# A two-layer hybrid decoder step: token rows of the expert stage by indirect transfers through DRAM tables

## The reference, cut to what matters

```
def swiglu(h, w_up, w_down):
    g, u = jnp.split(h @ w_up, 2, axis=-1)
    return (jax.nn.silu(g) * u) @ w_down

def moe_swiglu(h, w_router, w_up, w_down):
    logits = jnp.einsum('bld,de->ble', h, w_router, preferred_element_type=jnp.float32)
    top_v, top_i = lax.top_k(logits, TOP_K)
    top_w = jax.nn.softmax(top_v, axis=-1)
    combine = jnp.sum(top_w[..., None] * jax.nn.one_hot(top_i, N_EXPERTS, dtype=jnp.float32), axis=-2)
    ...
    for e in range(N_EXPERTS):
        out = out + combine[..., e:e + 1] * swiglu(h, w_up[e], w_down[e])
```

## Time and profile before

| | |
|---|---|
| median of three runs | 2266.97 us (2265.43 to 2270.44) |
| the profiled execution | 2268.26 us; span 2266.6 us |
| mean granted clock of TensorE | 0.992 of full speed |
| first expert slab asked for | 1306.66 us |
| expert products begin | 1320.29 us |
| last down product ends | 2252.7 us |
| DMA moved | 535.21 MB, mean 236 GB/s |

### The profile page before, as it was taken

How to read it: one execution, slowest core, us unless ns; L and a number is a source line. 1 busy time by engine, 2 the same in 40 slices (tenths; PEclk the granted TensorE clock), 3 DMA queues, 4 the chain that set the end, 5 groups by cost and what they waited for, 6 DMA issues and landing times.

```text
span 2266.6 us, 44485 instructions
## 1 busy us (share of the span) xinstructions
PE 2225.8 (98%) x19914; PEld 1410.3 (62%) x19914; DVE 621.5 (27%) x1229; ACT 386.3 (17%) x720; POOL 89.1 (4%) x138
## 2 busy tenths in 40 slices
PE   7999999999999999999999989999999999999999
PEld 6777777777777777777776744354444535353535
DVE  4394424432111128623353211111111020201011
ACT  3324333301000132342431110000000000000000
POOL 2001120000000000012000000000000000000000
PEclk9999999999999999999998999999999999999999
DMA  5335446464443543453476099999999899999993
GB/s 170 115 112 154 132 135 189 121 198 133 130 134 107 171 130 113 128 171 117 131 187 181 19 382 411 419 410 353 387 390 391 343 372 405 367 357 370 406 373 131
DMA packets 290397, 535.21 MB, mean 236 GB/s; under 512 B 10936, under 2 KB 222010, under 8 KB 273824
## 3 DMA queue, kind: packets, MB, share of 16 engines
q1 hardware_dynamic: 289836, 532.31, 66.5%
q10 hardware_dynamic: 372, 0.07, 0.0%
HBM read 518.50 MB, written 13.85 MB: 235 GB/s over the span
## 4 chain that ended last, share of the span: by engine, by line
PE 94%; DVE 3%; ACT 1%; issue 1%; DMA 1%; ACTq 0%; SPq 0%; DVEq 0%
PE bank L916 92%; PE bank L922 3%; ACT mem L1794 0%; DMA mem<-in_cache_kv_w_dram 0%; DVE mem L2521 0%; DVE col L2524 0%; DVE mem L2492 0%; DVE mem L2534 0%; DVE mem L2537 0%; ACTq L2103 0%; SPq L631 0%; DMA hv<-in_ssm_d_dram 0%; DVE mem L2213 0%; DVE mem L2217 0%; ACT hflat L1794 0%
## 5 line engine op out<-in xcount | busy, mean ns | idle before, releaser
L916 PE MATMUL bank<-mem 128*32 128x256 f32 (+10 forms) x11936 | 1033.7, 405 | 19.8 <-DVE mem L2860 5.4
L916 PEld LDWEIGHTS bank<-mem 128*32 128x32 f32 (+3 forms) x11936 | 606.2, 122 | 421.5 <-issue 231.6
L916 PE MATMUL bank<-hflat,mem 128*128 128x288 f32 (+1 forms) x2896 | 714.1, 407 | 0.0
L916 PEld LDWEIGHTS bank<-hflat,mem 128*128 128x128 f32 (+1 forms) x2896 | 536.0, 189 | 162.0 <-issue 19.3
L1794 ACT ACTIVATE mem<-bank 128x288 f32<-128x288 f32 (+8 forms) x384 | 171.2, 455 | 1135.3 <-PE bank L916 943.0
L916 PE MATMUL bank<-mem,steps 128*32 128x384 f32 (+1 forms) x3072 | 291.9, 539 | 0.0
L916 PEld LDWEIGHTS bank<-mem,steps 128*32 128x32 f32 x3072 | 98.6, 110 | 184.0 <-issue 183.2
L2213 DVE TENSOR_TENSOR xT<-xT,bank 128x288 f32<-128x288 f32 x72 | 28.4, 450 | 458.0 <-PE bank L916 458.0
L2217 DVE SCALAR_TENSOR_TENSOR mem<-mem,bank 128x288 f32<-128x288 f32 (+1 forms) x93 | 43.2, 479 | 214.7 <-ACT mem L1794 177.9
L1794 ACT ACTIVATE mem<-mem 128x1152 f32<-128x1152 f32 (+8 forms) x103 | 80.4, 780 | 100.3 <-DVE mem L2291 71.7
L922 PE MATMUL bank<-ident,mem 128*128 128x128 f32 (+3 forms) x570 | 80.0, 273 | 12.2 <-DMA mem<-in_x_sample_dram 7.1
(11 more groups left out here) (220 smaller groups left out, 749.2 us busy)
## 6 DMA issues: line engine op xcount, KB each, us to landing
mem<-in_w_moe_up_dram SPq DMA_DIRECT2D x64, 2048.0 KB, 11.2
mem<-in_w_moe_down_dram SPq DMA_DIRECT2D x56, 2048.0 KB, 11.2
mem<-in_w_moe_up_dram SPq DMA_DIRECT2D x32, 2304.0 KB, 9.7
mem<-in_w_in_dram SPq DMA_DIRECT2D x70, 1024.0 KB, 5.5
mem<-in_w_moe_up_dram SPq DMA_DIRECT2D x16, 1536.0 KB, 8.4
mem<-in_w_ffn_up_dram SPq DMA_DIRECT2D x44, 512.0 KB, 4.6
mem<-in_cache_kv_w_dram SPq DMA_DIRECT2D x26, 512.0 KB, 5.9
mem<-in_w_ffn_down_dram SPq DMA_DIRECT2D x16, 704.0 KB, 4.9
```

The lines of the kernel that those rows point to most:

```text
L916: return mm(out, lhsT, rhs, start=start, stop=stop, skip_group_check=True)
```

## The change

**Rows instead of matrices.** Two tables in DRAM, `xslots` and `yslots`, have 8 x 96 rows of 4 KB, one for each slot. DVE works out two slot numbers for each token (`to_slots`, 8 small instructions). POOL writes each token's normalised row to its two slots with six indirect DMAs (`put_rows`). ACT reads an expert's 96 rows with four DMAs (`load_rows`), DVE transposes them in 32 x 32 blocks to `hg` (`turn_expert`). The expert's output is stored to `yslots` with four DMAs (`store_rows`), and ACT waits until they have landed. When the last experts are done, POOL reads each token's two output rows back (`get_rows`: six DMAs while the last expert's down slabs run, three behind its store), and DVE adds them, weighted, to the residual in token rows `xrow`.

**What goes.** `gather`, `scatter`, the transposes of `Pc`, DVE's `Pm`, `Pc` and `add_scattered`, ACT's copies of `hg` and `Cm`, `turn_out` in the tail. The 24 transposes of `xT` now stand ahead of the loop (`turn_rows`), two blocks ahead of the rank products and one behind.

**What moves.** SP asks for expert slabs without knowing the number of rounds; each engine reads it inside the loop (`load_rounds` behind expert 0, on SP behind expert 1). PE raises `m_slab` by 16 ahead of the last branch projection of layer 1, which lets slabs 0 and 1 be asked for right behind the last `wo` slab, and by the other 5 behind the last `wo` product, which lets slabs 2 to 6 be asked for. In layer 0 SP fills the tables once (four DMAs, 3.5 MB from DRAM to DRAM), behind the stores of the key-value rows.

The diff, cut to its core (the bodies of `gather` and `scatter`, which go, stand in the code above):

```diff
+        hraw = view(arena, 3456, KT * CAP)
+        htok = view(arena, 6912, 3, D)
+        htokv = view(arena, 6912, 3, 4, KT * 32)
+        xrow = [xT[:, :, :].rearrange("p k t -> p (k t)")[:, D * b:D * b + D] for b in range(2)]
+        xrow.append(view(arena, 5888, D))
+        ylo = [eslot[0][:, 0:D], eslot[0][:, D:2 * D], eslot[1][:, 0:D]]
+        yhi = [eslot[0][:, 2 * D:3 * D], eslot[0][:, 3 * D:4 * D], eslot[1][:, D:2 * D]]
...
+        xslots = nc.dram_tensor("xslots", (NEXP * CAP, D), F32).ap()
+        yslots = nc.dram_tensor("yslots", (NEXP * CAP, D), F32).ap()
+        def slots_of(v, e):
+            return [v[CAP * e:CAP * e + CAP, 256 * q:256 * q + 256].rearrange("(p b) c -> p b c", b=TT) for q in range(4)]
+        def load_rounds(eng, end):
             eng.wait_ge(rounds_ready, 1)
-            return eng.value_load(rounds, min_val=1, max_val=-(-T // CAP))
+            eng.reg_load(end, rounds)
...
+                if L == 0:
+                    for i in range(3):
+                        sp.dma_start(xslots[TP * i:TP * i + TP, :], x_prompt[0]).then_inc(x_seeded, 16)
+                    sp.dma_start(yslots[CAP * (NEXP - 1):CAP * NEXP, :], x_prompt[0, 0:CAP, :]).then_inc(x_seeded, 16)
...
-            nr = load_rounds(sp)
-            with sp.Fori(0, nr) as r:
+            end = sp.alloc_register("sp_rounds")
+            with sp.Fori(0, end) as r:
...
+                    if e == 1:
+                        load_rounds(sp, end)
+                for b, (t0, n) in enumerate(BLK):
+                    dst = y_prompt[0, t0:t0 + n, :] if t0 < TP else y_sample.rearrange("b i d -> (b i) d")
+                    sp.wait_ge(y_added, 6 * r + 4 + b)
+                    sp.dma_start(dst, xrow[b][0:n, :]).then_inc(out_stored, 16)
...
+            def put_rows(dst, slots, src):
+                return gp.indirect_dma_start(dst, bass.IndirectOffsetOnAxis(ap=slots, axis=0), src, None,
+                                             bounds_check=last_row, oob_is_err=False)
...
+            pool.wait_ge(token_rstd, 1)
+            pool.wait_ge(tok_half0, 3)
+            for b, (t0, n) in enumerate(BLK):
+                half = htokv[0:n, b, :, 0:P]
+                step(gp.tensor_tensor(half, half, t_rstd[0:n, b:b + 1].unsqueeze(2).to_broadcast([n, 4, P]), ALU.mult))
...
+                pool.wait_ge(slots_ready, r + 1)
+                pool.sem_inc(pool_step, 1)
+                for b, (t0, n) in enumerate(BLK):
+                    for k in range(2):
+                        put_rows(xslots, slot_row[0:n, b, k:k + 1], htok[0:n, b, :]).then_inc(x_scattered, 16)
+                load_rounds(pool, end)
+                last = expert(r, NEXP - 1)
+                pool.wait_ge(y_out, 64 * last)
+                pool.wait_ge(*lat("m_slab", last, 16))
+                pool.sem_inc(pool_step, 1)
+                for b, (t0, n) in enumerate(BLK):
+                    get_rows(ylo[b][0:n, :], slot_row[0:n, b, 0:1], yslots).then_inc(lo_here[b], 16)
+                    get_rows(yhi[b][0:n, :], slot_early[0:n, b:b + 1], yslots).then_inc(hi_here[b], 16)
+                for b in range(3):
+                    pool.wait_ge(hi_here[b], 32 * r + 16)
+                    pool.sem_inc(pool_step, 1)
+                pool.wait_ge(y_out, 64 * last + 64)
+                pool.sem_inc(pool_step, 1)
+                for b, (t0, n) in enumerate(BLK):
+                    get_rows(yhi[b][0:n, :], slot_late[0:n, b:b + 1], yslots).then_inc(hi_here[b], 16)
...
+                if L == DEPTH - 1:
+                    pe.sem_inc(loop_signals["m_slab"], 16)
...
+            def turn_rows(b):
+                t0, n = BLK[b]
+                for k in range(2):
+                    acc = open_bank(("xrow", b, k))
+                    for i in range(4):
+                        ins = turn(acc[0:n, P * i:P * i + P], xT[:, 4 * k + i, t0:t0 + n])
+                    close_bank(ins, ("xrow", b, k))
             pe.wait_ge(*drained(("wo", 1, KT - 1)))
-            advance(pe, "m_slab")
+            pe.sem_inc(loop_signals["m_slab"], LOOP["m_slab"] - 16)
+            turn_rows(0)
+            turn_rows(1)
...
+            turn_rows(2)
+            for b in range(3):
+                for k in range(2):
+                    pe.wait_ge(*drained(("xrow", b, k)))
+            pe.wait_ge(*drained(("htok", 2, 1)))
...
-                        if n < 2 and e > 0:
-                            scatter(it - 1, n)
-                        if n == 2:
-                            pe.wait_ge(*lat("m_sel", it, 1))
-                            for b in range(TT):
-                                pe.wait_ge(*lat("m_added", it - 1, 5 + b))
-                                for tb, (t0, nt) in enumerate(BLK):
-                                    ins = turn(bank[up_bank[b]][:, t0:t0 + nt], Pc[0:nt, tb, b, :])
-                            ins.then_inc(*lup("m_turned"))
-                    pe.wait_ge(*lat("m_weights", it, TT))
+                    pe.wait_ge(*lat("m_hid", it - 1, 2 * TT))
...
-                        if n == 15 and e % 2 and e < NEXP - 1:
-                            gather_most(it + 1)
-                        if n == 18 and e % 2 and e < NEXP - 1:
-                            gather_rest(it + 1)
...
+            for b, (t0, n) in enumerate(BLK):
+                for k in range(2):
+                    key = ("xrow", b, k)
+                    copy_out(xrow[b][0:n, 512 * k:512 * k + 512], key, psum(key)[0:n, :])
...
+            def load_rows(e):
+                for q, src in enumerate(slots_of(xslots, e)):
+                    act.dma_start(hraw[32 * q:32 * q + 32, :].rearrange("p (b c) -> p b c", b=TT), src).then_inc(x_here, 16)
+            def store_rows(e):
+                for q, dst in enumerate(slots_of(yslots, e)):
+                    act.dma_start(dst, yb[32 * q:32 * q + 32, :, :]).then_inc(y_out, 16)
+            with act.Fori(0, end) as r:
+                act.wait_ge(x_scattered, 96 * (r + 1))
+                act.wait_ge(*lat("m_hgT", expert(r, 0) - 1, 1))
+                load_rows(0)
...
+                    if e < NEXP - 1:
+                        act.wait_ge(*lat("m_hgT", it, 1))
+                        load_rows(e + 1)
...
+                    act.wait_ge(*lat("m_y", it, 2))
+                    store_rows(e)
+                    act.wait_ge(y_out, 64 * it + 64)
...
+            def to_slots(step, done):
+                step(ve.tensor_scalar(near, rank2, 1.0, None, ALU.is_ge))
+                step(ve.scalar_tensor_tensor(near, rank2, float(CAP), near, ALU.is_le, ALU.mult))
+                step(tt(place, rank2, first_slot, ALU.add))
+                step(ve.scalar_tensor_tensor(slot_row, near, -OFF_END, place, ALU.mult, ALU.add))
+                step(tt(hi_at, place[:, :, 1], hi_7, ALU.add))
+                step(ve.scalar_tensor_tensor(slot_early, near[:, :, 1], -OFF_END, hi_at, ALU.mult, ALU.add))
+                step(ve.scalar_tensor_tensor(hi_at, place[:, :, 1], OFF_END, hi_7, ALU.add, ALU.subtract))
+                ins = ve.scalar_tensor_tensor(slot_late, near[:, :, 1], -OFF_END, hi_at, ALU.mult, ALU.add)
+                ins.then_inc(slots_ready, 1)
+                dve.wait_ge(slots_ready, done)
...
+                ve.scalar_tensor_tensor(xrow[b][0:n, :], rows[b][0:n, :], masked[0:n, b, k:k + 1], xrow[b][0:n, :],
+                                        ALU.mult, ALU.add).then_inc(y_added, 1)
...
+                def turn_expert(it, e):
+                    dve.wait_ge(x_here, 64 * (it + 1))
+                    ve.transpose(hg[e % 2].rearrange("p b k t -> p (b k t)"), hraw).then_inc(*lup("m_hgT"))
...
+                for b in range(3):
+                    dve.wait_ge(lo_here[b], 16 * (r + 1))
+                    add_expert(r, b, 0, ylo)
+                for b in range(3):
+                    dve.wait_ge(hi_here[b], 32 * (r + 1))
+                    dve.wait_ge(y_added, 6 * r + b + 1)
+                    add_expert(r, b, 1, yhi)
```

More of the change, by code:

```diff
@@ L45 @@
 CAP = 96
+OFF_END = 8192.0
 TT = CAP // 32
@@ L458, in hybrid_decoder @@
         for b in range(3):
[L459 to L460 removed]
+            for k in range(2):
+                job(("xrow", b, k), ((5, 6), (7, 3), (0, 1))[b][k])
         def filled(key):
@@ L1678, in _ @@
-            with pe.Fori(0, nr) as r:
-                gather_most(expert(r, 0))
-                gather_rest(expert(r, 0))
+            end = pe.alloc_register("pe_rounds")
+            with pe.Fori(0, end) as r:
                 for e in range(NEXP):
@@ L2130, in token_copies @@
                     key = ("htok", b, half)
-                    copy_out(htok[0:n, b, 512 * half:512 * half + 512], key, psum(key)[0:n, :])
+                    act.wait_ge(*filled(key))
+                    out = htokv[0:n, b, :, P * half:P * half + P].rearrange("t g (k f) -> t k g f", k=4)
+                    src = psum(key)[0:n, :].rearrange("t (k g f) -> t k g f", k=4, g=4)
+                    if half:
```

(17 more changed lines are left out.)

255 lines of the change are left out of this document (79 added, 176 removed).

## The result

The changed kernel takes 2232.85 us (median of four runs, 2230.22 to 2235.6) against 2266.51 for the kernel before beside it: a ratio of 0.9849, 95% interval 0.9831 to 0.9866. It is 34 us faster; 2219 was forecast, so the direction held and 14 us of the gain did not come. The profiled execution has a span of 2230.8 us, 35.8 less than before; by its own sum the prediction had 47.8 less.

A forecast was written before the change was run, and what follows sets the result against it. PE's own work was taken to bound the expert loop, with the feed close behind. Loop -62.0, rounds +1, head +11.8 and tail +1.4 gave -47.8 us from 2266.97: 2219 us, 8-in-10 range 2207 to 2240.

The forecast's parts named there:

- The loop: Expert loop: 62.0 us of gathers, scatters and transposes leave PE; 870.4 us left against 932.4, plus 1 us for rounds.
- (d): Head: rows landing beside slabs 2 to 6, forecast at 1325.5, between 1323 and 1333.
- (e): Head: ACT's four loads until 1329, DVE's turn 1.0 us; PE starts products at 1330.2, 9.9 us later than before.
- (a): Head: 16 transposes ahead of the rank products take 6.5 us, bounds 4.4 and 8.7; rank begins at 1308.2.
- (b): Head: rank products 2.2 us, then 11 small DVE instructions at 0.20 us; slots at 1312.8.
- (c): Head: six indirect DMAs on POOL at 1.3 us each, 7.8 us, last one out at 1320.6.
- (f): First products after PE's 18 us stop: 3.8 us at half speed, 1.9 us lost.
- The tail: Behind the expert loop: output stores, POOL's reads and DVE's multiply-add take 15.3 us, +1.4 against before.
- The filling of the tables: Layer 0: 3.5 MB read and written, 17 us at 415 GB/s, hidden behind wo slabs; nothing charged.
- The feed: Slab loading in the loop: 415 GB/s, rows cost 20 us in all, no stall; rival giving way a little 14%.
- 27 us to spare: Loop feed: 833 us needed of 860 us, so it holds while it keeps 402 GB/s.
- The sentence on the early request: Slabs asked for early: takes nothing off the path by itself, as PE did not wait for a slab before.

The follow-up runs named there:

- e3: Changed kernel without row loads for experts 1 to 7 and output stores of experts 0 to 6, early gets not waiting for stores: 2227.62 us, ratio 0.9827.
- e4: Changed kernel with the six early reads of yslots held until slab 20 instead of 16 of the last expert: 2232.35 us, ratio 0.9851.
- e1: Changed kernel with SP waiting for all six row puts before asking for the third slab of expert 0: 2228.82 us, ratio 0.9829.
- e9: Changed kernel with slabs 2 to 6 of the first expert asked for only after its rows are loaded: 2231.02 us, ratio 0.9846.
- e2: Changed kernel without the early request, all seven slabs asked for behind the last wo product: 2236.07 us, ratio 0.9864.
- e5: Changed kernel with PE doing only one row tile of each expert slab, all slabs and rows still moved: 2208.32 us (one run).

## Why the prediction was right or wrong

**The loop: right.** 62.0 us of gathers, scatters and transposes left PE, and nothing took their place: 870.2 us in e3 and 870.1 in e4 for 870.4 forecast, or 873.3 with the 1 us for the rounds and the 1.9 of slow clock. That clock is in the measured figures too, so the products themselves are some 3 us shorter than 8 x 108.8 (why is open), and reading the number of rounds costs nothing that shows. The changed kernel's own loop, 874.54 us, lies outside the 870 to 872 that the prediction named, by one late slab: 2.8 us of waiting and 1.6 of slow clock behind it.

**The head: step (d) failed**, and with it (e)'s start. The prediction put the rows' landing at 1325.5, between 1323 for the rows alone and 1333 for rows and slabs together. Behind the mark that is 28.0 us; it was 34.9. The steps ahead of it were too dear. (a) took 1.97 us, not 6.5: the prediction took eight records for four transposes, but a transpose of helper line 922 has one record, not two (a block's eight are x8 in the earlier trace rows, the sixteen are x16 at line 983 here), so its own row gives 2.2 us at full clock and not 4.4. In e1, e3 and e9, where the clock was still low, the sixteen took 3.7 us. (b) came out 4.6 us sooner behind the mark even though POOL's scaling held VectorE up for some 2 us, and (c) was right at 1.27 us each for 1.3. The last put went out 4 us ahead of the forecast and still landed 7 us behind it. No middle was to be taken: 12.9 MB asked for on common engines end together, and the upper bound, 1333 or 35.5 us behind the mark, was the answer (34.9). From the first put to the last landing the changed kernel took 23.3 us (1311.31 to 1334.57), e1 9.7 (1309.21 to 1318.92). The estimate by the Trainium skill for puts strictly in turn was 17.4; the trace does not agree, they overlap, and what makes them slow is what lies beside them. With loads and turn at 6.0 us for 4.7 PE started 40.91 us behind the mark instead of 32.7: 8.2 us.

**The clock after the stop, (f): right**, 2.6 us lost for 1.9. **The tail: right**, 15.66 for 15.3. **The filling of the tables: right**, no wait of PE from 440 to 700 us is for a DMA.

**The feed: price and rate right, reserve wrong.** 415 GB/s and 20 us for the rows stand (415.5 and 21.1). But "27 us to spare" was worked out as a surplus over the whole loop. Requests come at PE's pace, so engines that are ahead stand idle and can save nothing; what counts is how late a slab may be. Its landing was 12.1 us near 1400, and the last but one was waited for when it took 30.26, 2.8 too long: the reserve was 15 us. With rows and instructions beside them, slabs get 399.6 GB/s where PE takes 406.3; over 860 us that is 14 us, and the 2.1 MB of early reads, which the sum left out, are up to 5 more. The landing grew by 18. The forecast that SP's waits for PE would be far shorter than 810.9 us failed too: they are 714.1 + 47.3 us, since SP waits for a free slab at any landing time within the reserve.

**The sentence on the early request was wrong**: "takes nothing off the path by itself". By e2 it is worth 7.8 us at the start of the products and 3.8 at the end.

**The account.** On the spans 12.0 us of the forecast are missing: 8.2 the start of the products, 2.2 between the start of the span and the mark (run to run, as far as can be seen), 1.2 the loop (4.4 for the late slab, less 3.2 charged too much), 0.4 the tail.

## What to carry to other kernels

When a latency chain goes through DMAs, count everything that was asked for ahead of it on the same engines: it lands behind those bytes, whichever queue they are on. Hold back the requests that are not needed yet, but only as many as the feed's reserve allows; here three of five ahead gave 10 us, none of five gave nothing. And a ring's reserve is the time by which a slab may land late, not the feed's surplus over the loop.

## What was not expected of the hardware

- An indirect DMA of 128 rows holds POOL for 0.96 to 0.98 us (the first for 1.22), with 0.3 us ahead of the next. With no slab beside them (e1), the last of six has landed 3.17 us behind its issue.
- A wait of 2.8 us was enough for the granted clock to fall to 0.63 for the next 3.8 us; the late slab cost 4.4 us in all.
- Three POOL passes over 128 x 512 elements, both inputs in SBUF, made VectorE instructions of 0.2 us take about 1.05, as long as one pass; with the passes moved to ACT they took 0.17 to 0.21. The Trainium skill ("SBUF — State Buffer", "Who interferes with whom") says that the two engines share one way into SBUF for instructions with two inputs in SBUF, that forms of `tensor_scalar` can take it as well, and that the loser waits for the whole instruction. The trace agrees: one of the two shown has two inputs in SBUF, the other is a TENSOR_SCALAR.
- The instruction queue (q8) takes 0.7% of the DMA engines where PE does all its products (e9) and 0.2% where it does a third (e5). With the engines full, the slabs' share is lower by the same 0.5% (98.9% for 99.4%).
